# Loading x by blocks of channels, and turning it between the chunks of the projection

## The reference, cut to what matters

```
h = rmsnorm(x, g_mix)                       # x: 256 tokens x 1024 channels, float32
proj = h @ w_in                             # w_in: 1024 x 2048, columns [u | q | k | v], 512 each
y_pool = pooling mixer on u;  y_attn = dilated attention on q, k, v (8 heads)
x = x + concat(y_pool, y_attn) @ w_out
x = x + moe(rmsnorm(x))                     # 32 experts, the best 4 of each token, w_gu and w_down of all 32
return rmsnorm(x, g_final)
```

## Time and profile before

| | us |
|---|---|
| median of 3 runs | 1019.98 (1018.63 to 1020.21) |
| span of the profiled execution (first to last instruction) | 1018.5 |
| PE busy | 961.3 (94%) |
| DVE busy | 285.9 (28%) |
| ACT busy | 133.6 (13%) |
| mean transfer rate over the span | 412 GB/s |

### The profile page before, as it was taken

The page is one execution under the profiler, slowest core; times in us unless marked ns, Lnnn a source line. Parts: engine busy times, 40 slices in busy tenths (PEclk is TensorE's granted clock), DMA queues, the critical chain, the costliest instruction groups (busy, mean ns, idle before and its releaser), DMA issues.

```text
span 1018.5 us, 11652 instructions
## 1 busy us (share of the span) xinstructions
PE 961.3 (94%) x4851; PEld 423.1 (42%) x4851; DVE 285.9 (28%) x537; ACT 133.6 (13%) x200; POOL 15.1 (1%) x17
## 2 busy tenths in 40 slices
PE   8999999999998998989899898989899898999996
PEld 8988443434342342424243242424334342434332
DVE  5963531322222113112122212212211311222123
ACT  6634200000101000000001000000100000010002
POOL 0500000000000000000000000000000000000000
PEclk9999999999999899989999999999989998999998
DMA  9678999999999999999999999999999999999994
GB/s 353 220 329 365 411 426 420 431 426 431 430 434 432 428 429 430 423 430 435 427 432 432 429 431 427 430 436 434 431 429 426 429 432 431 433 427 432 425 425 200
DMA packets 26903, 419.63 MB, mean 412 GB/s; under 512 B 4228, under 2 KB 4888, under 8 KB 8920
## 3 DMA queue, kind: packets, MB, share of 16 engines
q1 hardware_dynamic: 26832, 419.15, 97.0%
q10 hardware_dynamic: 40, 0.01, 0.0%
HBM read 418.11 MB, written 1.05 MB: 412 GB/s over the span
## 4 chain that ended last, share of the span: by engine, by line
PE 55%; DMA 40%; DVE 3%; ACT 1%; issue 0%; SPq 0%; DVEq 0%
PE ps L1008 53%; DMA raw<-in_w_gu 37%; DMA raw<-in_w_down 3%; DVE woutl L736 1%; PE ps L1277 1%; PE ps L1332 1%; ACT sm L552 0%; PE ps L1019 0%; PE ps L1118 0%; DVE biased L931 0%; DVE mxs L753 0%; DVE sm L748 0%; DMA cst<-in_consts 0%; PE ps L1172 0%; DVE acc L987 0%
## 5 line engine op out<-in xcount | busy, mean ns | idle before, releaser
L1008 PE MATMUL ps<-raw,xT 128*64 128x512 f32 x2032 | 471.3, 614 | 44.4 <-DMA raw<-in_w_gu 44.0
L1008 PEld LDWEIGHTS ps<-raw,xT 128*64 128x64 f32 x2032 | 142.9, 141 | 344.2 <-issue 283.5
L1008 PE MATMUL ps<-raw,actT 128*64 128x512 f32 x1024 | 232.3, 595 | 0.9 <-DMA raw<-in_w_down 0.7
L1008 PEld LDWEIGHTS ps<-raw,actT 128*64 128x64 f32 x1024 | 70.5, 137 | 134.8 <-issue 129.4
L931 DVE TENSOR_TENSOR biased<-ps,biasT 128x1024 f32<-128x1024 f32 x32 | 39.2, 1225 | 294.7 <-PE ps L1277 294.7
L618 ACT ACTIVATE gu<-ps 128x1024 f32<-128x1024 f32 x32 | 32.8, 1025 | 526.1 <-PE ps L1008 526.1
L948 DVE TENSOR_TENSOR acc<-ps,acc 128x512 f32<-128x512 f32 x60 | 38.9, 687 | 175.8 <-PE ps L1008 175.8
L832 DVE TENSOR_TENSOR xT<-ps,gT 128x512 f32<-128x512 f32 x32 | 22.1, 692 | 166.0 <-PE ps L1008 165.8
L1008 PE MATMUL ps<-ysc,dispT 64*128 64x512 f32 x256 | 65.5, 613 | 0.0
L1008 PEld LDWEIGHTS ps<-disp,h 128*128 128x128 f32 x512 | 58.4, 192 | 12.4 <-issue 12.2
L1008 PE MATMUL ps<-disp,h 128*128 128x128 f32 x512 | 61.7, 278 | 0.2 <-DVE disp L826 0.2
(11 more groups left out here) (162 smaller groups left out, 445.6 us busy)
## 6 DMA issues: line engine op xcount, KB each, us to landing
raw<-in_w_gu SPq DMA_DIRECT2D x55, 4096.0 KB, 33.4
raw<-in_w_down SPq DMA_DIRECT2D x62, 2048.0 KB, 31.4
raw<-in_w_gu SPq DMA_DIRECT2D x16, 2048.0 KB, 12.3
win<-in_w_in SPq DMA_DIRECT2D x16, 512.0 KB, 14.0
wout<-in_w_out SPq DMA_DIRECT2D x4, 1024.0 KB, 9.4
raw<-in_w_down SPq DMA_DIRECT2D x4, 1024.0 KB, 36.1
early<-in_w_gu SPq DMA_DIRECT2D x1, 2048.0 KB, 11.5
raw<-in_w_gu SPq DMA_DIRECT2D x2, 1024.0 KB, 8.4
```

Source lines behind the costliest of these rows:

```text
L1008: return pe.matmul(out_, lhsT, rhs, start=start, stop=stop, skip_group_check=shared)
```

## The change

x is loaded in four blocks of 256 channels (all 256 tokens, so in pieces of 1 KB) instead of two tiles of 128 tokens. win[0][0] is loaded in two column halves, q's first; ACT and DVE split it in two halves too, so `win_low[0]` counts one more and chunk c waits for c+2. Blocks 1 to 3 of x are issued ahead of win[0][1], win[0][3] and win[0][5], and the constants go from behind win[0][1] to ahead of win[0][7]. PE turns block 0 before the first chunk, block 1 behind chunk 0, block 2 ahead of chunk 2 and block 3 ahead of chunk 4. The warm-up matmuls go from 8 and 10 to 3 and 5. The three semaphores of the stores at the end become one. ACT's list is the same but for the two halves and the wait for all four blocks ahead of the squares.

```diff
@@ block.sync
             sp.dma_start(cst[:, 0:P], consts[:, 0:P]).then_inc(ident_loaded, 16)
-            for t in range(TT):
-                sp.dma_start(acc[:, t, :], x[0, t * P:(t + 1) * P, :]).then_inc(x_loaded[t], 16)
+            def load_x(b):
+                cols = slice(b * 2 * P, (b + 1) * 2 * P)
+                sp.dma_start(acc[:, :, cols], x[0, :, cols].rearrange("(t p) n -> p t n", p=P)).then_inc(x_loaded[b], 16)
+
+            load_x(0)
+            sp.dma_start(win[0][0][:, DP:HALF], w_in[0, 0:P, DP:HALF]).then_inc(q_loaded, 16)
+            sp.dma_start(win[0][0][:, 0:DP], w_in[0, 0:P, 0:DP]).then_inc(win_loaded[0][0], 16)
             for h in range(2):
-                for c in range(DC):
+                for c in range(1 - h, DC):
+                    if h == 0 and c % 2:
+                        if c < DC - 1:
+                            load_x(c // 2 + 1)
+                        else:
+                            sp.dma_start(cst[:, P:N_CONST], consts[:, P:N_CONST]).then_inc(const_loaded, 16)
                     sp.dma_start(win[h][c][:, :], w_in[0, c * P:(c + 1) * P, h * HALF:(h + 1) * HALF]).then_inc(
                         win_loaded[h][c], 16)
-                    if h == 0 and c == 1:
-                        sp.dma_start(cst[:, P:N_CONST], consts[:, P:N_CONST]).then_inc(const_loaded, 16)
...
@@ block.scalar
             turned_high(0)
-            win_part(0, 0)
+            act.wait_ge(q_loaded, 16)
+            act.activation(winh[0][0][:, DP:HALF], win[0][0][:, DP:HALF], ACT.Copy).then_inc(win_high[0], 1)
+            act.wait_ge(win_loaded[0][0], 16)
+            act.activation(winh[0][0][:, 0:DP], win[0][0][:, 0:DP], ACT.Copy).then_inc(win_high[0], 1)
             win_part(0, 1)
             turned_high(1)
             win_part(0, 2)
...
             win_part(0, 4)
+            for b in range(DC // 2):
+                act.wait_ge(x_loaded[b], 16)
             for t in range(TT):
-                act.wait_ge(x_loaded[t], 16)
                 act.activation(junk[t][:], acc[:, t, :], ACT.Square, accum_out=ssq[:, t:t + 1]).then_inc(squares, 1)
...
@@ block.tensor
             pe.wait_ge(ident_loaded, 16)
-            for _ in range(8):
+            def turn_x(b):
+                pe.wait_ge(x_loaded[b], 16)
+                for c in (2 * b, 2 * b + 1):
+                    for t in range(TT):
+                        ins = pe.transpose(ps[:, b, (c % 2) * T + t * P:(c % 2) * T + (t + 1) * P],
+                                           acc[:, t, c * P:(c + 1) * P], c_("ident"))
+                ins.then_inc(x_turned, 1)
+
+            for _ in range(3):
                 mm(ps[:, 4, 0:P], c_("ident"), c_("ident"))
+            turn_x(0)
             pe.wait_ge(vec_loaded, 48)
...
-            for _ in range(10):
+            for _ in range(5):
                 mm(ps[:, 5, 0:P], c_("ident"), c_("ident"))
             pe.wait_ge(vec_ready, 1)
             pe.wait_ge(hTh_ready, 1)
-            pe.wait_ge(win_high[0], 1)
             first_chunk(((6, DP), (4, 0)))
+            turn_x(1)
             for c in range(1, DC):
+                if c in (2, 4):
+                    turn_x(c // 2 + 1)
                 pe.wait_ge(hTl_ready, c // 2 + 1)
-                pe.wait_ge(win_low[0], c + 1)
+                pe.wait_ge(win_low[0], c + 2)
```

More of the change, by code:

```diff
@@ L237, in bc @@
             return ap.broadcast_to(list(dims))
-        x_loaded = [sem(f"x_loaded{t}") for t in range(TT)]
+        x_loaded = [sem(f"x_loaded{b}") for b in range(DC // 2)]
         half_used = sem("half_used")
@@ L251, in hybrid_layer @@
         win_loaded = [[sem(f"win_loaded{h}{c}") for c in range(DC)] for h in range(2)]
+        q_loaded = sem("q_loaded")
         ident_loaded, const_loaded, vec_loaded, wout_loaded = (
@@ L259, in hybrid_layer @@
         out_weighted, out_ready = sem("out_weighted"), [sem(f"out_ready{n}") for n in range(TT + 1)]
-        stored = [sem(f"stored{n}") for n in range(TT + 1)]
+        stored = sem("stored")
         squares, inv_ready, rstd_ready, scaled = sem("squares"), sem("inv_ready"), sem("rstd_ready"), sem("scaled")
@@ L449, in _ @@
             sp.wait_ge(out_ready[0], 2)
-            sp.dma_start(out[0, 0:P, :], outs[:, 0, :]).then_inc(stored[0], 16)
+            sp.dma_start(out[0, 0:P, :], outs[:, 0, :]).then_inc(stored, 16)
             for h in range(2):
                 sp.wait_ge(out_ready[1 + h], 1)
-                sp.dma_start(out[0, P:T, h * 512:(h + 1) * 512], outs[:, 1, h * 512:(h + 1) * 512]).then_inc(stored[1 + h], 16)
-            for n in range(TT + 1):
-                sp.wait_ge(stored[n], 16)
+                sp.dma_start(out[0, P:T, h * 512:(h + 1) * 512], outs[:, 1, h * 512:(h + 1) * 512]).then_inc(stored, 16)
+            sp.wait_ge(stored, 16 * (TT + 1))
         @block.gpsimd
@@ L686, in win_rest @@
             def win_rest(h, c):
-                dve.wait_ge(win_high[h], c + 1)
+                dve.wait_ge(win_high[h], c + 2 - h)
                 dve.tensor_tensor(winl[h][c][:, :], win[h][c][:, :], winh[h][c][:, :].bitcast(F32),
@@ L700, in _ @@
             turned_low(0)
-            win_rest(0, 0)
+            for n, cols in enumerate((slice(DP, HALF), slice(0, DP))):
+                dve.wait_ge(win_high[0], n + 1)
+                dve.tensor_tensor(winl[0][0][:, cols], win[0][0][:, cols], winh[0][0][:, cols].bitcast(F32),
+                                  ALU.subtract).then_inc(win_low[0], 1)
             win_rest(0, 1)
@@ L1040, in first_chunk @@
                         pe.wait_ge(hTl_ready, 1)
-                    if product == 2:
-                        pe.wait_ge(win_low[0], 1)
-                    for bank, column in parts:
+                    for n, (bank, column) in enumerate(parts):
+                        if product != 1:
+                            pe.wait_ge((win_low if product else win_high)[0], n + 1)
                         for j in range(4):
```

## The result

The changed kernel takes 1023.16 us (median of 5 runs, 1022.94 to 1025.86) against 1020.06 before. The ratio is 1.0039, with a 95% interval of 1.0028 to 1.0049: slower by 4 us. (The means of the five runs on either side lie 4.1 us apart, the medians 3.1.) The forecast was 1025.6 in a range of 1022.8 to 1028.5.

A forecast was written before the change was run, and what follows sets the result against it. Expert-weight loads, which wait for PE, bound the kernel, so attention-stage delays pass on. PE's gain of 2.5 us at chunk 1 became a lag, DVE's uT came 5.6 us late: 1019.98 + 5.6 = 1025.6 us, range 1022.8 to 1028.5.

The forecast's parts named there:

- The place and the direction: Loss from PE's idle time ahead of chunk 4 and the work queued behind it on ACT and DVE; slower, chance 0.88.
- The start: PE up to chunk 1: chunk 0 at about 7.3, chunk 1 at 12.0 instead of 14.50, 2.5 us gained.
- The middle: Chunks 2 to 7: PE idles about 3.3 us ahead of chunk 4, squares 6.4 us later, uT at 41.0.
- Behind it: After uT: six woutl stay at 1.9 us each beside POOL's sums, kT at 53.5 without waiting for PE.
- the 5.6 us: Forecast delay of uT on DVE, 41.0 instead of 35.37, added whole to the median time.
- Rival 1: Half clock after PE's idle times; hidden behind chunk 4, but scores 1.7 to 2.8 us later: 1027.3 to 1028.4; chance 0.09.
- 2.9 us of cover: PE sums u at about 38.1, 2.9 us ahead of DVE, so PE's stalls up to that cost nothing more.
- The second idle time that rival 1 feared: PE idle 2.2 us between v's first two chunks, ending at 52.5, and kT at 54.7, ahead of the scores.
- the low end of the range: Lower bound of the 8 in 10 range, 1022.8, for a delay half as long as worked out, +2.8 us.
- Small transfers: Loads at the start: six 256 KB pieces move more slowly, everything 1 to 2 us later, 1026.6 to 1027.6; chance 0.06.
- Taken up later: Expert loading after the attention stage has room and absorbs the delay, about 1020 to 1021 us; chance 0.06.
- Not slower: ACT keeps its lead and the early start pays, at most 1018.3 us, 0.16% faster; chance 0.05.

The follow-up runs named there:

- run 4: The kernel before with only the last four transposes of x (block 3) moved behind chunk 3; 1023.76 us, ratio 1.0041.
- run 1: The changed kernel with block 3 of x turned ahead of chunk 3 instead of chunk 4; 1019.47 us, ratio 0.9998.
- run 8: The changed kernel, block 3 turned ahead of chunk 3, ACT's and DVE's lists in arrival order, POOL's window sums held until kT; 1018.41 us, ratio 0.9984.
- run 6: The kernel before with POOL's window sums held back until kT is written; 1019.37 us, ratio 0.9993.
- run 3: The changed kernel with two changes of ACT's function table ahead of the first wouth, making woutl late; 1026.36 us, ratio 1.0064.
- run 7: The changed kernel with block 3 turned ahead of chunk 3 and ACT's and DVE's lists in arrival order; 1019.38 us, ratio 0.9994.
- run 2: The changed kernel with 14 matmuls of the identity filling PE's wait between block 3 and chunk 4; 1022.98 us, ratio 1.0031.
- run 9: The kernel before with POOL's window sums waiting only for DVE's first woutl; 1020.20 us, ratio 0.9999.
- run 10: The changed kernel, block 3 turned ahead of chunk 3, lists in arrival order, POOL's window sums waiting for DVE's first woutl; 1019.79 us, ratio 0.9999.
- run 5: The changed kernel run once more, unchanged, against the kernel before; 1024.03 us, ratio 1.0044.

## Why the prediction was right, and which step was off

**The place and the direction** were right and are now shown. The move of block 3 alone gives 1.0041 (run 4), putting it one chunk earlier alone gives 0.9998 (run 1). What else is in the change comes, all together, to nothing that these runs can tell; gains and costs inside that sum are not separated.

**The start.** Forecast and trace: chunk 0 at 7.3 and 7.86, its end at 10.9 and 11.1, chunk 1 at 12.0 and 12.0. (The forecast's own terms, 7.3 + 2.96 + 0.8, make 11.1 and not 10.9; nothing hangs on it, since chunk 1 waits for its weights.) The start does give PE 2.5 us at chunk 1. What reaches the end when nothing takes it back is much less: kT at 45.80 in run 8 against 46.42 in run 6, both with POOL held back, and 1018.41 against 1019.37 us (the intervals of their ratios overlap, so a gain by the start is likely and not shown).

**The middle.** The last hTh at 22.3 and 22.35, chunk 4 at 25.4 and 25.54, squares at 24.0 and 24.02, uT at 41.0 and 40.93. Chaining durations from the rows of before, instruction by instruction, through the fixed lists of three engines was enough for this.

**Behind it, the term that was mis-sized.** The forecast said: "The six woutl take 1.9 us each [...] since POOL sums the windows of uT at that time; POOL starts on uT too, so this moves along." It didn't move along. woutl started 1.13 us apart, the row of six took 6.90 us instead of 11.4, so DVE gave back 4.5 of the 5.6 us. What was left was PE's own delay. The forecast had u summed 2.8 us late; the load that SP issues on it went out at 39.26 against 35.29, 4.0 us late, of which the half clock is some 1.5 us (16 matmuls at 0.21 instead of 0.12). PE's transposes of the probabilities start 3.4 us late (64.71 against 61.28). Rival 1 said that a half clock behind chunk 4 would be hidden under 2.9 us of cover. At uT it still was hidden, but at kT DVE waited 1.83 us for PE, so there the cover didn't exist; the row of PE from 25.54 on has no wait in it that could have hidden it. The second idle time that rival 1 feared, at the scores, didn't come for the same reason. Run 3 gives the counterproof: with woutl slow again PE waits 1.6 us for kT and the time is 1026.36.

**The number.** That the time fell inside the range is in part luck. The 5.6 us that gave 1025.6 did not reach the end; the measured 4 us are another quantity, PE's lag, and the low end of the range, 1022.8, stood for a delay only half as long and not for this.

**The other rivals.** Small transfers: win[0][1] landed at 9.5 against the 9.6 forecast, chunk 1 started at 12.0 as forecast, and run 1 is level with before. Taken up later: the loads follow PE as before. Not slower: 1018.3 was the most that an early start could give, and run 8 comes to 1018.41, with other lists and with POOL held back; in what part the start does it is open.

**What stays open.** The change's ratio gives 4 us, the two profiled spans 2.6. For the change the profiled execution was the fastest of its five runs. In every run whose span is recorded the time lies 1.7 to 1.9 us above the span; by that the profiled execution of the kernel before took about 1020.3 us, an estimate, which is as slow as its slowest run. Single runs of the change reach 1025.9. A run in which POOL gets the port would look so (run 3), but no profile caught one, and there is a rival: the mean granted clock of the runs of 1025.86 and 1025.92 is 0.974, under the 0.976 to 0.978 of run 3's, so that more time at half clock may be behind them. How much the half clock costs by itself is not settled: run 2 didn't separate it from the longer slow pitch at the start.

## What to carry to other kernels

When a producer's work is spread among a consumer's steps, look at what stands behind the waiting instruction on every engine between them: here PE postponed four transposes, 0.4 us of work, and ACT's fixed list had PE's next weights queued behind them. Move the consumer's list along with the producer's, or leave the producer's step where it was; putting first what arrives first brought uT from 37.79 (run 1) to 34.63 (run 7), though not a time that can be told. And when a stretch of an engine is slow because of a neighbour, don't carry the slow duration to another time: ask who holds the shared thing at that moment, and keep the fast duration as the other bound.

## What was unexpected in the hardware

**Who gets the port that DVE and POOL share.** DVE's subtraction with both inputs in SBUF (1.22 us alone) and POOL's window sum (1.99 us alone in run 3) shut each other out. In the change POOL's first sum asked at 42.29 (that is where its record starts) and ended 1.85 us behind the end of the sixth woutl (48.96): it was recorded with 8.52 us, most of them waiting. In the kernel before it asked at 36.73 and ended 1.85 us behind the first woutl (37.72), and the second woutl, which waited for it, took 3.02 us. So the same two lists give 6.9 or 11.4 us for six woutl. Operations of DVE that read PSUM, as kT, took 1.21 to 1.23 us in either case. The Trainium skill, "SBUF — State Buffer", section "SBUF: two separate sides", says that the pair of ports is an exclusive lock, held for a whole instruction by whoever starts first. The traces agree, and add that POOL can be kept out for six instructions of DVE.

What decides between the two outcomes is not shown. A rule suggests itself: POOL stands back when the input of DVE's next woutl is already there as it asks, and gets in when it isn't. In the kernel before the second wouth was ready at 37.30, after POOL had asked; in the change it was ready at 41.78, before. Ten of the twelve profiles fit: POOL's first sum got in before, and in runs 3, 7, 9 and 10, and stood back in the change and in runs 1, 2, 4 and 5. Runs 6 and 8 don't fit. In run 6 the last wouth was ready at 43.3, POOL asked at 47.88 while the seventh woutl ran, and still went ahead of the eighth, which took 3.02 us:

```profile
41.31 2.01 ACT L544 ACTIVATE wouth<-wout 128x1024 fp32r<-128x1024 f32 x2 [0.55 <-DMA wout<-in_w_out]
47.88 2.75 POOL L476 TENSOR_TENSOR wsA<-uT 128x1084 f32<-128x1084 f32 x1 [18.56 <-DVE kT L728]
48.69 3.02 DVE L737 TENSOR_TENSOR woutl<-wout,wouth 128x1024 fp32r<-128x1024 f32 x1
```

POOL's second sum in the kernel before doesn't fit either: it asked at 39.65, when the third wouth had been ready since 38.26, and went ahead of the third woutl, which took 2.55 us. Whoever plans with such a pair can only give both outcomes, or keep the two apart as run 6 did for the first six.

**The pitch at the start.** The first stretch of slow pitch (0.21 us from matmul to matmul, against 0.12 behind it) ended at 8.5 us in one profile of the change and at 10.6 in the other, and only at about 12.2 in run 2. Over the eight profiles with the short warm-up it ended between 7.7 and 12.2 us, over the four with the long one between 7.4 and 8.7. The view by stretches gives a granted clock of 1.00 for all of it, so that it is the clock is an inference from the pitch, which is that of the stretch at 0.50 behind chunk 4. With the short warm-up the time at which chunk 0 runs at full speed is a matter of the execution. The wait of 3.2 us ahead of chunk 4 brought a granted clock of 0.50 in two of the four profiles that have it.
